# Feed-forward blocks of a two-part transformer: the first weight slice loaded a stage ahead, the gate folded into the down weights, and partition sums as float32r products

## The chip, the cores and the metric

The kernel runs on one core of a Trainium2 chip (trn2). The metric is device time in microseconds for one execution. A core has five engines with queues of their own: TensorE (PE, with its weight loads as PEld), VectorE (DVE), ScalarE (ACT), GpSimd (POOL) and SyncE (SP), which here issues most of the DMA transfers.

## What is computed

Two transformer parts run one after the other on 512 tokens of width 1024, in float32. The change touches the feed-forward block, which occurs twice in the first part, once behind a mixer of RWKV type (i = 0) and once behind one with sparse attention (i = 1):

```
def _swiglu(h, w_in, w_out):
    gate, up = jnp.split(h @ w_in, 2, axis=-1)
    return (jax.nn.silu(gate) * up) @ w_out
...
for i in range(DEPTH):
    mod = cond @ ada_w[i] + ada_b[i]
    sh1, sc1, gt1, sh2, sc2, gt2 = jnp.split(mod[:, None, :], 6, axis=-1)
    ...
    x = _layernorm(DEEPNORM_ALPHA * x + (1 + gt1) * y, ln_g[i, 0], ln_b[i, 0])
    hin = x * (1 + sc2) + sh2
    y = _swiglu(hin, ffn_w_in[i], ffn_w_out[i])
    x = _layernorm(DEEPNORM_ALPHA * x + (1 + gt2) * y, ln_g[i, 1], ln_b[i, 1])
```

The hidden width is 2816, that is 22 slices of 128. `cond` is silu of a vector of 1024, so `mod` is a matrix-vector product with a matrix of 1024 x 6144.

## The kernel before

The program is a row of stages: projections, chunks and end of the RWKV mixer ("proj", "chunks", "mixed"), feed-forward ("ffn0"), attention ("dsa"), feed-forward ("ffn1"), then the second part with "hyb" and the experts. Between two stages stands a barrier of all engines. `stay` holds the tiles that outlive a stage. Within a stage every engine has a list of its own, written by hand, and semaphores tie them together; the order on an engine is the order of the code.

Float32 products run as three float32r products: each operand is split into a high part (a cast) and a low part (`low_half`, a subtraction), and `matmul_halves` adds high x high, low x high and high x low (lines 49 to 51).

`swiglu` does one feed-forward block:

- **Input.** TensorE transposes `x` into eight chunks, ScalarE scales and shifts them (line 300, `xT`), VectorE splits them (lines 381 and 43). Between the fourth and the fifth chunk (`FIRST = 3`) both engines take in the first slice's weights (`cast_in`, `split_in`).
- **Gate and up.** For each slice n of 128 hidden columns SP loads 1 MB of weights (`load_in`, two transfers, line 169), ScalarE casts them (line 296), VectorE makes the low half, TensorE runs 2 x 8 x 3 products of 128x512, ScalarE applies silu (line 312), VectorE multiplies and splits the result (`gate_up`, lines 361, 363, 43). Weights have two buffers, `wi[0]` and `wi[1]`.
- **The next modulation.** Beside this the block computes `mod` of the layer that follows, in 24 pieces of 256 columns. SP loads 1 MB per piece (line 163), VectorE sums 8 terms into `nsum` and adds the bias on one partition (`next_piece`, lines 371 to 377), TensorE sums over the partitions with a product against a column of ones (`next_sum`, line 230), ScalarE copies the row out and stores it. The first pair of slices (`pair(0)`) handles two pieces per slice, the loop behind it one.
- **Down.** 22 slices of `w_out`, 0.5 MB each, go through a ring of four buffers (line 198). VectorE casts and subtracts (`split_out`, lines 351 and 43). Eight PSUM banks collect 4 quarters of tokens x 2 halves of columns. Up to slice 17 TensorE takes all quarters of a slice, the last four slices quarter by quarter.
- **End.** `deepnorm_rows` works off the quarters on VectorE: gate times bank (line 431), plus ALPHA times x (432), moments (434), normalisation (439, 440). The mixers end with the same function.

The down buffers lie on the same memory as the gate/up buffers.

## Time and profile before

| | us |
|---|---|
| median of 3 runs | 2979.43 |
| the runs | 2970.38, 2979.43, 2979.59 |
| profiled execution, own time | 2968.92 |
| its span, first to last instruction | 2967.2 |
| busy in it: TensorE / VectorE / ScalarE | 2613.1 / 1962.0 / 908.8 |
| first feed-forward block | 639 to 1051 |
| second feed-forward block | 1376 to 1791 |

Times in rows count from the span's start. A row of the timeline gives start, duration, engine, line, operation, what is written and read, and in brackets the idle time before it with what ended it. Rows of one engine can overlap a little, since a duration includes the way through the pipeline; the step from start to start is what counts. Busy time is an average over many stages; what a change in a stage is worth shows in who waits for whom there. In row names both feed-forward blocks read `ffn`.

### The profile page before, as it was taken

How to read it: one execution, taken by the hardware profiler on the slowest of the kernel's cores; microseconds unless marked ns; L12 is line 12 of the kernel's file. 1: busy time of each engine (PE TensorE's matmuls, PEld its weight loads, DVE VectorE, ACT ScalarE, POOL GpSimd, SP SyncE). 2: the span in 40 equal slices, each digit the busy share in tenths (PEclk: the TensorE clock that was granted, in tenths of full speed). 3: DMA queues.
4: the chain of work that ended last, by engine and by line, in shares of the span. 5: the costliest groups of instructions: out<-in, count | busy, mean ns of one | idle time of the engine just before them, and what ended most of it. 6: DMA issues, size and time to landing. Idle time of an engine off the chain costs nothing. (4 is left out here: it accounts for less than half of the span.)

```text
span 2967.2 us, 41251 instructions
## 1 busy us (share of the span) xinstructions
PE 2613.1 (88%) x16553; PEld 1913.8 (65%) x16553; DVE 1962.0 (66%) x2648; ACT 908.8 (31%) x961; POOL 409.6 (14%) x214
## 2 busy tenths in 40 slices
PE   5999888869999979996999996998882899999991
PEld 3444888447778744663777875885432688888880
DVE  7580666777764538526776457976524799999983
ACT  2201111122220022522222003333101677777761
POOL 0000000100000010000000000000001266666642
PEclk8999999989999989998999998999995899999995
DMA  5210222226663270102665323220306699999962
GB/s 186 85 57 18 93 74 74 115 92 199 186 182 99 85 252 29 58 29 93 202 188 175 100 85 112 87 86 29 142 8 218 237 361 368 369 359 360 355 246 102
DMA packets 241388, 459.54 MB, mean 155 GB/s; under 512 B 30966, under 2 KB 193294, under 8 KB 225897
## 3 DMA queue, kind: packets, MB, share of 16 engines
q1 hardware_dynamic: 220344, 432.09, 41.9%
q0 software_dynamic: 14368, 23.79, 2.3%
q10 hardware_dynamic: 6546, 1.79, 0.3%
q8 instruction: 99, 1.62, 0.2%
q14 instruction: 31, 0.25, 0.0%
HBM read 457.49 MB, written 30.56 MB: 164 GB/s over the span
## 5 line engine op out<-in xcount | busy, mean ns | idle before, releaser
L49 PE MATMUL ffn_bank<-ffn_xT_high,ffn_wi_high 128*128 128x512 f32 x704 | 281.2, 399 | 20.7 <-ACT ffn_xT L300 18.2
L50 PE MATMUL ffn_bank<-ffn_xT_low,ffn_wi_high 128*128 128x512 f32 x704 | 275.9, 392 | 0.0
L51 PE MATMUL ffn_bank<-ffn_xT_high,ffn_wi_low 128*128 128x512 f32 x704 | 275.9, 392 | 0.0
L296 ACT CAST ffn_wi_high<-ffn_wi 128x2048 fp32r<-128x2048 f32 x44 | 84.0, 1910 | 355.1 <-DMA ffn_wi<-in_ffn_w_in 320.9
L49 PEld LDWEIGHTS ffn_bank<-ffn_xT_high,ffn_wi_high 128*128 128x128 f32 x704 | 133.3, 189 | 66.1 <-ACT ffn_xT L300 18.6
L374 DVE SCALAR_TENSOR_TENSOR ffn_nsum<-ffn_nw,ffn_cond,ffn_nsum 128x256 f32<-128x256 f32 x336 | 163.0, 485 | 12.0
L2810 POOL DMA_INDIRECT expert_rows<-exp_ys,exp_to_row x32 | 155.6, 4863 | 45.1 <-issue 44.3
L43 DVE TENSOR_TENSOR moe_g_low<-moe_g,exp_g_high 128x4096 fp32r<-128x4096 f32 x32 | 141.6, 4425 | 30.0 <-ACT exp_g_high L2884 30.0
L43 DVE TENSOR_TENSOR ffn_wi_low<-ffn_wi,ffn_wi_high 128x2048 fp32r<-128x2048 f32 x44 | 100.8, 2291 | 79.9 <-ACT ffn_wi_high L296 79.9
L51 PEld LDWEIGHTS ffn_bank<-ffn_xT_high,ffn_wi_low 128*128 128x128 f32 x704 | 133.3, 189 | 28.7
L2884 ACT CAST exp_g_high<-moe_g 128x4096 fp32r<-128x4096 f32 x32 | 116.3, 3634 | 113.1 <-PE exp_p_g L51 83.6
L43 DVE TENSOR_TENSOR moe_u_low<-moe_u,exp_u_high 128x4096 fp32r<-128x4096 f32 x32 | 141.6, 4426 | 13.6 <-ACT exp_u_high L2884 13.6
L50 PEld LDWEIGHTS ffn_bank<-ffn_xT_low,ffn_wi_high 128*128 128x128 f32 x704 | 133.3, 189 | 26.5
L43 DVE TENSOR_TENSOR moe_d_low<-moe_d,exp_d_high 128x4096 fp32r<-128x4096 f32 x32 | 141.4, 4419 | 0.0
L49 PE MATMUL ffn_bank<-ffn_wo_high,ffn_act_high 128*128 128x512 f32 x352 | 137.4, 390 | 2.4 <-DVE ffn_wo_low L43 2.4
L50 PE MATMUL ffn_bank<-ffn_wo_low,ffn_act_high 128*128 128x512 f32 x352 | 137.0, 389 | 0.0
L51 PE MATMUL ffn_bank<-ffn_wo_high,ffn_act_low 128*128 128x512 f32 x352 | 137.0, 389 | 0.0
L2884 ACT CAST exp_d_high<-moe_d 128x4096 fp32r<-128x4096 f32 x32 | 116.5, 3642 | 2.1 <-DMA moe_d<-in_w_e_down 2.1
L2794 POOL COPY exp_from_row<-exp_rows 128x2 int32 (+1 forms) x30 | 113.9, 3796 | 19.4 <-PE exp_p_x L2839 19.2
L351 DVE CAST ffn_wo_high<-ffn_wo 128x1024 fp32r<-128x1024 f32 x44 | 30.5, 694 | 129.9 <-DMA ffn_wo<-in_ffn_w_out 129.9
L2884 ACT CAST exp_u_high<-moe_u 128x4096 fp32r<-128x4096 f32 x32 | 116.4, 3636 | 0.0
L49 PE MATMUL exp_p_g<-exp_g_high,exp_xT_high 128*128 128x512 f32 x256 | 105.6, 412 | 8.4 <-DVE exp_xT_low L43 8.4
(608 smaller groups left out, 5937.7 us busy)
## 6 DMA issues: line engine op xcount, KB each, us to landing
moe_g<-in_w_e_gate SPq DMA_DIRECT2D x32, 2048.0 KB, 9.5
moe_u<-in_w_e_up SPq DMA_DIRECT2D x32, 2048.0 KB, 10.0
moe_d<-in_w_e_down SPq DMA_DIRECT2D x32, 2048.0 KB, 9.3
ffn_wi<-in_ffn_w_in SPq DMA_DIRECT2D x88, 512.0 KB, 5.2
ffn_nw<-in_ada_w SPq DMA_DIRECT2D x24, 1024.0 KB
ffn_nw<-in_w_ada SPq DMA_DIRECT2D x24, 1024.0 KB
ffn_wo<-in_ffn_w_out SPq DMA_DIRECT2D x44, 512.0 KB, 3.3
hyb_wb<-in_w_in SPq DMA_DIRECT2D x20, 1024.0 KB, 5.9
```

What stands on the lines that cost most here:

```text
L43: return engine.tensor_tensor(low, x, high.bitcast(F32), ALU.subtract)
L49: nc.tensor.matmul(out, w[0], x[0], start=start, stop=False, **kw)
L50: nc.tensor.matmul(out, w[0], x[1], start=False, stop=False, **kw)
L51: return nc.tensor.matmul(out, w[1], x[0], start=False, stop=stop, **kw)
L296: nc.scalar.copy(wi_high[h][:, :, :, :], wi[h][:, :, :, :]).then_inc(s["wi_highs"], 1)
L351: nc.vector.tensor_copy(wo_high[slot][:, :], wo[slot][:, :]).then_inc(s["wo_highs"], 1)
L374: nc.vector.scalar_tensor_tensor(out=total, in0=nw[:, b, k, :], scalar=cond[:, k:k + 1], in1=total, op0=ALU.mult, op1=ALU.add).then_inc(s[ ...
L2794: nc.gpsimd.tensor_copy(from_row[h][:, :, :], rows[:, bass.ds(n, 1), :]).then_inc(s["from_copied"], 1)
L2810: nc.gpsimd.indirect_dma_start(ys_dram, bass.IndirectOffsetOnAxis(ap=to_row[h][:, 0, 1:2].bitcast(U32), axis=0), ys[h][:, :], None, bounds ...
L2884: nc.scalar.copy(flat(high_of(name, h)[:, :, :]), flat(raw[name][h][:, :, :])).then_inc(s[f"{name}_high"], 1)
```

## The change

Three things, all in the feed-forward blocks:

1. A tile `z` (8 KB per partition, float32, with `z_r` as its float32r view) joins `stay` and takes the place of `wi[0]`. The stage ahead of each block loads the first slice's weights into it: the last stage of the RWKV mixer behind its other loads, the attention stage behind its output weights and a wait on `prep_psum`. Other stages keep tiles of their own in `z` (`kk` and `sq`, `RBB`, `w_uk` and `w_uv`, a third ring buffer, `xg`). ScalarE and VectorE take in slice 0 ahead of all eight chunks.
2. The partition sum becomes two float32r products with 128x128 ones; VectorE makes `nsum_high` and `nsum_low` for it.
3. The gate plus one is formed at the start of the block and multiplied into each slice of down weights; `deepnorm_rows` skips its multiplication there. The rooms move: the first two down buffers and `g`, `b` lie on `nw` now, so their loads wait for the last piece (`nsum_done`).

```diff
+def load_first_slice(engine, stay, w_in, z_loaded):
+    for part in range(2):
+        engine.dma_start(first_slice(stay["z"])[:, part, :, :],
+                         w_in.rearrange("(p k) n -> p k n", k=KD)[:, :, part * FFN:part * FFN + P]).then_inc(z_loaded, 16)
...
-                load_in(0, 0)
                 load_in(1, 1)
                 load_piece(0, 0)
                 load_piece(1, 1)
...
-                    if f == 0 or f == 2:
-                        sp.wait_ge(s["hidden"], 2 * (NF - 1) + f)
-                        sp.wait_ge(s["wi_split"], NF - 1 + f // 2)
+                    if f == 0:
+                        sp.wait_ge(s["nsum_done"], PIECES + 1)
+                    if f == 2:
+                        sp.wait_ge(s["hidden"], 2 * NF)
...
-                pool.dma_start(gt[:, :], spread(gate)).then_inc(s["v_loaded"], 16)
+                pool.dma_start(gt[:, :], spread(gate)).then_inc(s["gt_loaded"], 16)
+                pool.wait_ge(s["nsum_done"], PIECES + 1)
                 pool.dma_start(g[:, :], spread(ln_g)).then_inc(s["v_loaded"], 16)
...
-                    nc.tensor.matmul(bank[4 + b][0:1, 0:PIECE], ones[:, :], nsum[:, b, :], start=True, stop=True).then_inc(s["n_psum"], 1)
+                    nc.tensor.matmul(bank[4 + b][:, 0:PIECE], ones[:, :], nsum_high[:, b, :], start=True, stop=False)
+                    nc.tensor.matmul(bank[4 + b][:, 0:PIECE], ones[:, :], nsum_low[:, b, :], start=False, stop=True).then_inc(s["n_psum"], 1)
...
+                cast_in(0, 0)
                 for k in range(KD):
                     act.wait_ge(s["xT_psum"], k + 1)
...
-                    if k == FIRST:
-                        cast_in(0, 0)
...
                     dve.wait_ge(wo_loaded[slot], f // WO_RING * 16 + 16)
+                    nc.vector.tensor_tensor(wo[slot][:, :], wo[slot][:, :], gt[:, :], ALU.mult).then_inc(s["wo_gated"], 1)
+                    dve.wait_ge(s["wo_gated"], f + 1)
                     nc.vector.tensor_copy(wo_high[slot][:, :], wo[slot][:, :]).then_inc(s["wo_highs"], 1)
...
-                    nc.vector.tensor_tensor(total[0:1, :], total[0:1, :], nbias[:, b, :], ALU.add).then_inc(s["nsum_done"], 1)
+                    nc.vector.tensor_tensor(total[0:1, :], total[0:1, :], nbias[:, b, :], ALU.add).then_inc(s["nsum_biased"], 1)
+                    dve.wait_ge(s["nsum_biased"], p + 1)
+                    nc.vector.tensor_copy(nsum_high[:, b, :], total).then_inc(s["nsum_high"], 1)
+                    dve.wait_ge(s["nsum_high"], p + 1)
+                    low_half(nc.vector, nsum_low[:, b, :], total, nsum_high[:, b, :]).then_inc(s["nsum_done"], 1)
...
+                split_in(0, 0)
                 for k in range(KD):
...
                 split_in(1, 1)
+                dve.wait_ge(s["gt_loaded"], 16)
+                link(nc.vector.tensor_scalar(gt[:, :], gt[:, :], 1.0, None, ALU.add))
...
@@ deepnorm_rows
-            link(nc.vector.tensor_tensor(y[:, t, cols], bank_of(t, j)[:, :], gt[:, cols], ALU.mult))
-            link(nc.vector.scalar_tensor_tensor(out=y[:, t, cols], in0=x[:, t, cols], scalar=ALPHA, in1=y[:, t, cols],
+            branch = bank_of(t, j)[:, :]
+            if gt is not None:
+                link(nc.vector.tensor_tensor(y[:, t, cols], branch, gt[:, cols], ALU.mult))
+                branch = y[:, t, cols]
+            link(nc.vector.scalar_tensor_tensor(out=y[:, t, cols], in0=x[:, t, cols], scalar=ALPHA, in1=branch,
                                                 op0=ALU.mult, op1=ALU.add))
...
@@ rwkv_finish, SP
             sp.dma_start(x_first, x_in.rearrange("(t p) d -> p t d", p=P)).then_inc(loaded, 16)
+            load_first_slice(sp, stay, next_w_in, z_loaded)
...
@@ dsa, SP
                 sp.dma_start(w_out, w["w_out"].rearrange("(q p) n -> p q n", p=P)).then_inc(ring_loaded[1], 16)
+                sp.wait_ge(s["prep_psum"], 18)
+                load_first_slice(sp, stay, next_w_in, z_loaded)
                 sp.wait_ge(s["o_psum"], KD)
```

ScalarE at the start of a feed-forward block, before (`ffn_xT` are the chunks of the input, `ffn_wi_high` the cast weights):

```order
L300 ACTIVATE ffn_xT<-ffn_bank,stay_sh,stay_sc 128x512 x4
L296 CAST ffn_wi_high<-ffn_wi 128x2048
L300 ACTIVATE ffn_xT<-ffn_bank,stay_sh,stay_sc 128x512 x4
L305 ACT_TABLE_LOAD
L305 ACTIVATE ffn_sig<-ffn_cond 128x8
L296 CAST ffn_wi_high<-ffn_wi 128x2048
```

and after:

```order
L319 CAST ffn_wi_high<-stay_z 128x2048
L324 ACTIVATE ffn_xT<-ffn_bank,stay_sh,stay_sc 128x512 x8
L327 ACT_TABLE_LOAD
L327 ACTIVATE ffn_sig<-ffn_cond 128x8
L319 CAST ffn_wi_high<-ffn_wi 128x2048
```

The first cast has moved from the middle of the chunks ahead of them, and reads `z`.

VectorE at the same place, from the last chunk through the first two pieces, before:

```order
L381 CAST ffn_xT_high<-ffn_xT 128x512
L43 TENSOR_TENSOR ffn_xT_low<-ffn_xT,ffn_xT_high 128x512
L43 TENSOR_TENSOR ffn_wi_low<-ffn_wi,ffn_wi_high 128x2048
L387 TENSOR_TENSOR ffn_cond<-ffn_cond,ffn_sig 128x8
L371 TENSOR_SCALAR ffn_nsum<-ffn_nw,ffn_cond 128x256
L374 SCALAR_TENSOR_TENSOR ffn_nsum<-ffn_nw,ffn_cond,ffn_nsum 128x256 x7
L377 TENSOR_TENSOR ffn_nsum<-ffn_nsum,ffn_nbias 1x256
L371 TENSOR_SCALAR ffn_nsum<-ffn_nw,ffn_cond 128x256
L374 SCALAR_TENSOR_TENSOR ffn_nsum<-ffn_nw,ffn_cond,ffn_nsum 128x256 x7
L377 TENSOR_TENSOR ffn_nsum<-ffn_nsum,ffn_nbias 1x256
```

and after, the first of the two pieces:

```order
L410 CAST ffn_xT_high<-ffn_xT 128x512
L43 TENSOR_TENSOR ffn_xT_low<-ffn_xT,ffn_xT_high 128x512
L43 TENSOR_TENSOR ffn_wi_low<-ffn_wi,ffn_wi_high 128x2048
L414 TENSOR_SCALAR ffn_gt<-ffn_gt 128x1024
L416 TENSOR_TENSOR ffn_cond<-ffn_cond,ffn_sig 128x8
L395 TENSOR_SCALAR ffn_nsum<-ffn_nw,ffn_cond 128x256
L398 SCALAR_TENSOR_TENSOR ffn_nsum<-ffn_nw,ffn_cond,ffn_nsum 128x256 x7
L401 TENSOR_TENSOR ffn_nsum<-ffn_nsum,ffn_nbias 1x256
L403 CAST ffn_nsum_high<-ffn_nsum 128x256
L43 TENSOR_TENSOR ffn_nsum_low<-ffn_nsum,ffn_nsum_high 128x256
```

The gate's plus one has come in ahead of `cond`, and a cast and a subtraction end every piece.

TensorE between slices 0 and 1, before:

```order
L50 MATMUL ffn_bank<-ffn_xT_low,ffn_wi_high 128x512
L51 MATMUL ffn_bank<-ffn_xT_high,ffn_wi_low 128x512
L230 MATMUL ffn_bank<-ffn_nsum,ffn_ones 1x256 x2
L49 MATMUL ffn_bank<-ffn_xT_high,ffn_wi_high 128x512
L50 MATMUL ffn_bank<-ffn_xT_low,ffn_wi_high 128x512
```

and after:

```order
L51 MATMUL ffn_bank<-ffn_xT_high,stay_z_r 128x512
L249 MATMUL ffn_bank<-ffn_nsum_high,ffn_ones 128x256
L250 MATMUL ffn_bank<-ffn_nsum_low,ffn_ones 128x256
L249 MATMUL ffn_bank<-ffn_nsum_high,ffn_ones 128x256
L250 MATMUL ffn_bank<-ffn_nsum_low,ffn_ones 128x256
L49 MATMUL ffn_bank<-ffn_xT_high,ffn_wi_high 128x512
```

Two float32r products stand where one fp32 product stood, for each of the two pieces here.

## Rows read from the trace of the kernel before

**Rows 1.** The page's header: the span of the profiled execution.
```profile
span 2967.2 us, 41251 instructions
```
**Rows 2.** Timeline of ScalarE, first block, around the first cast of weights.
```profile
647.82 1.90 ACT L296 CAST ffn_wi_high<-ffn_wi 128x2048 fp32r<-128x2048 f32 x1 [3.98 <-DMA ffn_wi<-in_ffn_w_in]
649.63 2.78 ACT L300 ACTIVATE ffn_xT<-ffn_bank,stay_sh,stay_sc 128x512 f32<-128x512 f32 x4
```
**Rows 3.** Timeline of VectorE, first block: its waits up to slice 2.
```profile
641.32 0.43 DVE L381 CAST ffn_xT_high<-ffn_xT 128x512 fp32r<-128x512 f32 x1 [1.70 <-ACT ffn_xT L300]
...
649.75 2.29 DVE L43 TENSOR_TENSOR ffn_wi_low<-ffn_wi,ffn_wi_high 128x2048 fp32r<-128x2048 f32 x1 [4.09 <-ACT ffn_wi_high L296]
...
679.28 2.29 DVE L43 TENSOR_TENSOR ffn_wi_low<-ffn_wi,ffn_wi_high 128x2048 fp32r<-128x2048 f32 x1 [1.35 <-ACT ffn_wi_high L296]
```
**Rows 4.** Timeline of VectorE, second block: the wait for the first weights.
```profile
1389.86 2.29 DVE L43 TENSOR_TENSOR ffn_wi_low<-ffn_wi,ffn_wi_high 128x2048 fp32r<-128x2048 f32 x1 [7.97 <-ACT ffn_wi_high L296]
```
**Rows 5.** Timeline of TensorE, first block: its waits, and a late partition sum.
```profile
652.46 0.79 PE L49 MATMUL ffn_bank<-ffn_xT_high,ffn_wi_high 128*128 128x512 f32 x1 [6.59 <-ACT ffn_xT L300]
...
667.48 0.59 PE L230 MATMUL ffn_bank<-ffn_nsum,ffn_ones 128*1 128x256 f32 x2 [1.98 <-DVE ffn_nsum L377]
...
694.33 0.50 PE L49 MATMUL ffn_bank<-ffn_xT_high,ffn_wi_high 128*128 128x512 f32 x1 [0.88 <-DVE ffn_wi_low L43]
...
879.93 0.59 PE L230 MATMUL ffn_bank<-ffn_nsum,ffn_ones 128*1 128x256 f32 x2
...
880.45 0.50 PE L49 MATMUL ffn_bank<-ffn_xT_high,ffn_wi_high 128*128 128x512 f32 x1
880.79 0.39 PE L50 MATMUL ffn_bank<-ffn_xT_low,ffn_wi_high 128*128 128x512 f32 x1
```
**Rows 6.** Windows: us, PE busy (count), granted clock, DMA share, GB/s.
```profile
655.00:657.00 2.00, 2.00 (x9) 0.91 1.10 349
669.00:670.00 1.00, 1.00 (x4) 0.51 0.93 266
670.00:672.00 2.00, 2.00 (x6) 0.50 1.03 350
```
**Rows 7.** Timeline, stage "hyb": float32r products of 128x256 and a weight load.
```profile
1910.03 0.28 PE L50 MATMUL hyb_bank<-hyb_wb_low,stay_h_high 128*128 128x256 f32 x1
1910.03 0.19 PEld L51 LDWEIGHTS hyb_bank<-hyb_wb_high,hyb_hT_low 128*128 128x128 f32 x1
1910.14 0.28 PE L51 MATMUL hyb_bank<-hyb_wb_high,hyb_hT_low 128*128 128x256 f32 x1
```
**Rows 8.** Groups by line and shape, VectorE: busy us, mean ns of one.
```profile
L351 DVE CAST ffn_wo_high<-ffn_wo 128x1024 fp32r<-128x1024 f32 x44 | 30.5, 694 | 129.9 <-DMA ffn_wo<-in_ffn_w_out 129.9
L381 DVE CAST ffn_xT_high<-ffn_xT 128x512 fp32r<-128x512 f32 x16 | 6.7, 421 | 3.4 <-ACT ffn_xT L300 3.4
L43 DVE TENSOR_TENSOR ffn_wo_low<-ffn_wo,ffn_wo_high 128x1024 fp32r<-128x1024 f32 x44 | 53.9, 1225 | 1.5
L43 DVE TENSOR_TENSOR ffn_xT_low<-ffn_xT,ffn_xT_high 128x512 fp32r<-128x512 f32 x16 | 11.1, 692 | 0.5
L374 DVE SCALAR_TENSOR_TENSOR ffn_nsum<-ffn_nw,ffn_cond,ffn_nsum 128x256 f32<-128x256 f32 x336 | 163.0, 485 | 12.0
```
**Rows 9.** Timeline: VectorE's tail, first block; TensorE's last wait, second block.
```profile
1019.96 0.69 DVE L431 TENSOR_TENSOR ffn_y<-ffn_bank,ffn_gt 128x512 f32<-128x512 f32 x1 [0.35 <-PE ffn_bank L51]
...
1027.71 0.68 DVE L431 TENSOR_TENSOR ffn_y<-ffn_bank,ffn_gt 128x512 f32<-128x512 f32 x1
...
1759.06 0.50 PE L49 MATMUL ffn_bank<-ffn_wo_high,ffn_act_high 128*128 128x512 f32 x1 [1.24 <-DVE ffn_wo_low L43]
```
**Rows 10.** Timeline of VectorE, first block, steady slices.
```profile
729.00 0.69 DVE L361 TENSOR_TENSOR ffn_hid<-ffn_sil,ffn_bank 128x512 f32 x1 [0.52 <-PE ffn_bank L51]
...
880.23 0.69 DVE L361 TENSOR_TENSOR ffn_hid<-ffn_sil,ffn_bank 128x512 f32 x1 [1.46 <-PE ffn_bank L51]
...
888.24 2.29 DVE L43 TENSOR_TENSOR ffn_wi_low<-ffn_wi,ffn_wi_high 128x2048 fp32r<-128x2048 f32 x1 [1.69 <-ACT ffn_wi_high L296]
```

More of the change, by code:

```diff
@@ L104, in swiglu @@
     WO_RING = 4
-    FIRST = 3
     STEADY = NF - WO_RING
@@ L111, in swiglu @@
         room = Room(nc, ctx, phase)
-        nw = room.sb("nw", [P, 2, KD, PIECE])
         xT_high, y = room.shared(("xT_high", [P, KD, T], F32R), ("y", [P, NT, D], F32))
@@ L478, in rwkv_project @@
     hid = room.sb("hid", [P, 2, T])
-    kk = room.sb("kk", [P, 2, T])
-    sq = room.sb("sq", [P, 2, T])
+    kk, sq = (stay["z"][:, n * 2 * T:(n + 1) * 2 * T].rearrange("p (a t) -> p a t", a=2) for n in range(2))
     nrm = room.sb("nrm", [P, 2, T])
@@ L866, in rwkv_chunks @@
     MK = room.sb("MK", [P, 2, KD, 2, CHUNK])
-    RBB = room.sb("RBB", [P, 2, KD, 2, CHUNK])
+    RBB = stay["z"][:, :].rearrange("p (e q k t) -> p e q k t", e=2, q=KD, k=2)
     ZA = room.sb("ZA", [P, 2, KD, 2, CHUNK])
@@ L1903, in hybrid @@
         xn = sgb[:, :, :].rearrange("p (t a) n -> p t (a n)", t=NT)
-        *third, hm = room.shared(("wb2", [P, KD, WB], F32), ("wb_low2", [P, KD, WB], F32R), ("hm", [P, NT, M_INNER], F32))
+        third = [stay[n][:, :].rearrange("p (k n) -> p k n", k=KD) for n in ("z", "z_r")]
+        hm = stay["z"][:, :].rearrange("p (t n) -> p t n", t=NT)
         wb, wb_low = zip(*raw_low, third)
@@ L2722, in experts @@
     rows = room.sb("rows", [P, UNITS, 2], I32)
-    xg = [room.sb(f"xg{i}", [P, D]) for i in range(2)]
+    xg = [stay["z"][:, i * D:(i + 1) * D] for i in range(2)]
     xT_high = room.sb("xT_high", [P, KD, P], F32R)
@@ L3064, in two_blocks @@
                                            ("h_high", [P, KD, T], F32R), ("x", [P, NT, D], F32))))
+        stay.update(zip(("z", "z_r"), room.shared(("z", [P, 2 * KD * P], F32), ("z_r", [P, 2 * KD * P], F32R))))
+        z_loaded = [nc.alloc_semaphore(f"z_loaded{n}") for n in range(2)]
         stay.update(ident=room.sb("ident", [P, P]), sc=room.sb("sc", [P, KD]), sh=room.sb("sh", [P, KD]))
```

63 lines of the change are left out of this document (36 added, 27 removed).

## Prediction

> **What bounds the kernel now.** The page's header comes first: one execution spans 2967.2 us [rows 1]. The change works in the two feed-forward blocks, from 639 to 1051 us and from 1376 to 1791 us, so only they are read. The question in each is who makes whom wait, and it has three answers.
>
> At the start TensorE waits. ScalarE converts the first slice's weights between the fourth and the fifth chunk of the transposed input; that conversion waits for a load that was only issued when the block began, and the last four chunks stand behind it [rows 2]. TensorE's first product starts at 652.46 after 6.59 us of waiting [rows 5]. VectorE waits too: 1.70 us for the first chunk, 4.09 us for the first converted weights, 1.35 us for those of slice 2 [rows 3]. In the second block the load takes longer, and the middle wait is 7.97 us [rows 4]; the other two are as in the first, 1.70 and 1.39. But look at what TensorE waits for next: at 667.48 for VectorE's partition sum of piece 1, and at 694.33 for VectorE's low half of slice 3's weights [rows 5]. The loop's first pair does two pieces per slice instead of one, and up to slice 3 the limit is VectorE's own queue.
>
> From slice 3 on TensorE is the limit. VectorE's gate step at the end of a slice stands at 729.00 and 13 slices later at 880.23, which is 11.63 us per slice. The low half of the next weights starts at 888.24 and takes 2.29, so it is done at 890.5, some 1.5 us before TensorE begins on it at about 892 [rows 10].
>
> At the end VectorE is the limit: each quarter of the tokens costs it 1027.71 - 1019.96 = 7.75 us [rows 9], while TensorE needs 4 x 6 products of about 0.23 us, 5.4 us.
>
> **Part 1, the early load.** The wait of ScalarE goes, and the conversion (1.90) comes ahead of the eight chunks instead of among them: it ends at about 641.3, the chunks go at 0.70 apiece (2.78 for four [rows 2]), so TensorE can start at about 647.0, 5.5 us earlier; in the second block some 9. That is not the gain. Up to slice 3 VectorE decides, so I add up VectorE's queue. It loses the waits of 4.09 and 1.35 us. The latter goes because slice 2's load is issued behind piece 1, which is done earlier, while VectorE arrives with more work behind it. The 1.70 stays, now as the wait for ScalarE's conversion. Added is, in each of six pieces before slice 3, a cast and a subtraction of 128x256. No row shows either on this tile. Cast: 0.421 for 512 and 0.694 for 1024 elements give 0.285 for 256. Subtraction: 0.692 and 1.225 give 0.425; the nearest row of this size, with a scalar, is 0.485 [rows 8]. With 0.03 for each new wait on the step before, 0.77 per piece, 4.6 for six; bounds 0.5 (both hidden in part behind the previous step's end) and 1.1 (0.421 + 0.692). The gate's plus one, 0.69 + 0.03, now also stands there. So slice 3 starts by -4.09 - 1.35 + 4.6 + 0.72 = **-0.1 us** in the first block and -7.97 - 1.39 + 5.3 = **-4.0 us** in the second. What hides the second slice's load is that it is now first in SP's queue, with 1 MB less ahead and 1 MB (scale and shift of the norm) moved to the block's end; if it still landed as late as 1387.9, some 1.5 us of the 4.0 would go.
>
> TensorE's waits do not vanish, they move. Piece 1 comes only 4.09 - 0.72 - 1.54 = 1.8 us earlier, while slice 0 ends over 5 us earlier; and before slice 3 the wait of 0.88 [rows 5] grows to about 2.9, since slice 2 starts up to 1.8 earlier and slice 3's weights come when they came before. After a wait of 1.98 us (667.48) the granted clock fell to 0.51 at 669 and stayed at 0.50 to 672 [rows 5, 6]: some 3.2 us at 1.2 GHz instead of 2.4, a loss of 1.6. The wait of 0.88 had none behind it. I expect such a stretch in slice 3 of both blocks, where nothing covers it: **+3.2 us**, bounds 0 and 6.4 (twice as long).
> On this the Trainium skill (TensorE: Matmul & The Clock Gate, HAM oscillation) says that a burst behind a long wait for data starts at the half rate again; by that rule the 3.2 stand, without it the sum would be 3.2 lower. The row at 669 agrees with it.
>
> The two extra DMA issues stand at the end of SP's queue in the mixer's last stage, behind everything it loads, and in the attention stage behind the output weights, with only a reload of the input behind them that waits for much later work. I cost them at nothing; 1 MB among 8, if it held up the x load, would be 3 to 5 us once, and VectorE takes x up tens of us later.
>
> **Part 2, partition sums as float32r.** Today one fp32 product with one column of weights runs as two instructions: from 879.93 to the next slice's product 0.52 us, which itself is followed by the next only after 0.34 [rows 5]. After, two products of 128x256 in float32r. The mixer of the second block runs such products at 0.11 apart, with their 128x128 weight loads alongside [rows 7]. Of the 0.52 some 0.43 is array time and becomes 0.23: 0.20 saved, with bounds 0 and 0.31 (if the slow first product behind it goes too). It counts where TensorE is the limit, behind slices 3 to 21, 19 times in each block: **-7.6 us**, bounds 0 and -11.8. The 20 or so slices each give VectorE 0.77 more; it has 1.46 us of idle time before the gate step and 1.69 before the low half [rows 10], so TensorE hides it.
> Against this part speaks a rule of the Trainium skill (TensorE: Matmul & The Clock Gate, LDWEIGHTS): a weight load costs by its columns, so 128 columns instead of 1. If the two loads stood in the open at the 0.107 us that it gives, an estimate from that page, the saving would be nil and the sum 7.6 higher. The rows of the 128x256 stream show them hidden.
>
> **Part 3, the gate in the down weights.** VectorE gets 22 more multiplications of 128x1024, 1.225 each [rows 8]: 3.2 us per slice of weights instead of 1.9, against TensorE's 5.4. Hidden, except for the last one: slice 21's load is issued only when TensorE leaves slice 17, and TensorE already waits 1.24 us for its low half [rows 9]. That wait grows by 1.23 + 0.03: **+2.5 us** over two blocks. The scale's plus one leaves this place, but it lay in that wait. In return the tail loses eight multiplications per block, each 0.69 with 0.03 to the step that depends on it, 0.72 [rows 9]: **-11.6 us** for sixteen. VectorE then takes 6.3 us per quarter and is still behind TensorE's 5.4, so all of it counts. The step that now reads PSUM keeps its length: the multiplication, which read the bank, took as long. The loads of the first two down slices come earlier, into the room of the next modulation's weights; TensorE did not wait for them before, so nothing.
>
> **The sum** is -4.1 + 3.2 - 7.6 + 2.5 - 11.6 = **-17.6 us**. The profiled execution took 2968.9 (span 2967.2 and 1.7 around it), so 2951.3 on its terms. The three timed runs were 2970.4, 2979.4 and 2979.6: the profiled one lies at the lower end. Against the median of 2979.4 the forecast is **2962 us**; if most runs fall on the lower level, 2953.
>
> **Rivals.** *The start pays in full* (0.10): VectorE's queue isn't the limit up to slice 3, and TensorE keeps its 5.5 and 9. For it: ScalarE's wait is the visible one. Against it: TensorE's waits at 667.48 and 694.33, both for VectorE. Then the start gives -14.5 instead of -0.9: 2948.
> *The small products and steps give nothing* (0.15): the weight loads stand open, or the added VectorE steps cost 1.1 instead of 0.77 (+2 per block, and slice 3 later still). Then -17.6 + 7.6 + 4 = -6: 2973, no difference that can be told.
> *Slower, by the clock* (0.05): behind the longer waits of both first slices TensorE stays at 1.2 GHz for a whole slice of 48 products, 10.9 us more each, instead of 1.6. In slice 1 about 3 of that is covered by VectorE's work, in slice 3 nothing: some 8 + 10.9 per block, 38 in all, less the 21 that the other terms give: +17, 2996. It decides from the point where the low stretches cost more than the other terms give, 10 us per block. Against it: after the wait of 6.59 us that ended at 652.46 the granted clock was back at 0.91 between 655 and 657, and the stretch from 669 ends behind 672 [rows 5, 6].
>
> **Numbers.** The forecast has 0.70. The range from 2946 to 2973 takes in the lower level of the runs with the full start, and the case in which the small steps give nothing. About 0.3%, 9 us, is what a measurement of this kernel can tell from no change: faster 0.82, same 0.13, slower 0.05.
>
> **What the profile after would show.** Right: the first product near 647 (first block), TensorE waiting 5 us for the sum of piece 1 and near 3 us for slice 3's low half, slice 3 starting within 1 us of 694.3; a step from slice to slice of 11.4 instead of 11.63 us; two and a half us of wait for the last down slice; a tail quarter of 6.3. Wrong: slice 3 near 689 (the first rival), slices still 11.6 apart (the second), a granted clock of 0.5 for whole slices (the third). A wait of the tail for TensorE would make part 3 worth less.

## The result, and the profile after

| us | before | after |
|---|---|---|
| median of the timed runs | 2979.43 | 2952.51 |
| lowest run | 2970.38 | 2945.45 |
| profiled execution, own time | 2968.92 | 2955.74 |
| its span | 2967.2 | 2954.0 |
| first block, start to end | 411.59 | 400.26 |
| second block, start to end | 415.56 | 401.47 |
| attention stage between them | 324.6 | 334.6 |

The ratio after to before is 0.9915, 95% interval 0.9893 to 0.9937: about 25 us faster (19 to 32). One of the five runs after, 4086.52 us at a mean granted clock of 0.614 where the others have 0.94, is a slow run and left out of the ratio; the median of the other four is 2949.0. On another chip 11 runs before and 6 after gave medians of 2970.03 and 2950.02, ratio 0.9936 (0.9924 to 0.9948), which is 20 us. In the profiled pair the two blocks give 11.33 + 14.09 = 25.4 us, and the attention stage, which the change doesn't touch, takes 10.0 back; the experiments show that this is not the change.

The page's header:
```profile
span 2954.0 us, 41412 instructions
```
The start. Timelines of ScalarE and VectorE, first block (start, duration, engine, line, operation, idle time before it); compare [rows 2, 3]:
```profile
640.33 1.90 ACT L319 CAST ffn_wi_high<-stay_z 128x2048 fp32r<-128x2048 f32 x1 [4.14 <-PEq L86]
642.13 5.76 ACT L324 ACTIVATE ffn_xT<-ffn_bank,stay_sh,stay_sc 128x512 f32<-128x512 f32 x8
```
```profile
642.26 2.29 DVE L43 TENSOR_TENSOR stay_z_r<-stay_z,ffn_wi_high 128x2048 fp32r<-128x2048 f32 x1 [1.53 <-ACT ffn_wi_high L319]
...
655.19 0.69 DVE L414 TENSOR_SCALAR ffn_gt<-ffn_gt 128x1024 f32<-128x1024 f32 x1
...
660.59 0.29 DVE L403 CAST ffn_nsum_high<-ffn_nsum 128x256 fp32r<-128x256 f32 x1
660.92 0.43 DVE L43 TENSOR_TENSOR ffn_nsum_low<-ffn_nsum,ffn_nsum_high 128x256 fp32r<-128x256 f32 x1
...
692.76 2.29 DVE L43 TENSOR_TENSOR ffn_wi_low<-ffn_wi,ffn_wi_high 128x2048 fp32r<-128x2048 f32 x1
```
The weights are there: ScalarE converts them first and takes the eight chunks in a row. VectorE has no bracket behind 642.26: it never waits up to slice 3, its queue is full. TensorE, first block, its waits; compare [rows 5]:
```profile
647.95 0.50 PE L49 MATMUL ffn_bank<-ffn_xT_high,ffn_wi_high 128*128 128x512 f32 x1 [1.10 <-ACT ffn_xT L324]
...
666.55 0.58 PE L249 MATMUL ffn_bank<-ffn_nsum_high,ffn_ones 128*128 128x256 f32 x1 [4.64 <-DVE ffn_nsum_low L43]
...
695.10 0.50 PE L49 MATMUL ffn_bank<-ffn_xT_high,ffn_wi_high 128*128 128x512 f32 x1 [2.68 <-DVE ffn_wi_low L43]
```
Counted from the block's start its first product comes 5.5 us earlier (7.56 us into the block instead of 13.05), and it gives this back at 666.55 and 695.10. In the second block the wait before slice 3 is as long, but the clock falls behind it. Windows (us, TensorE busy and count, granted clock, DMA share, GB/s): first block, second block:
```profile
697.00:700.00 3.00, 3.00 (x14) 1.00 1.11 328
1432.00:1434.00 2.00, 2.00 (x7) 0.50 1.09 307
```
The steady slices. TensorE from one slice to the next, and VectorE's gate steps (both first block); compare [rows 5, 10]:
```profile
762.70 0.39 PE L51 MATMUL ffn_bank<-ffn_xT_high,stay_z_r 128*128 128x512 f32 x1
762.93 0.28 PE L249 MATMUL ffn_bank<-ffn_nsum_high,ffn_ones 128*128 128x256 f32 x1
763.04 0.28 PE L250 MATMUL ffn_bank<-ffn_nsum_low,ffn_ones 128*128 128x256 f32 x1
763.16 0.39 PE L49 MATMUL ffn_bank<-ffn_xT_high,ffn_wi_high 128*128 128x512 f32 x1
763.39 0.39 PE L50 MATMUL ffn_bank<-ffn_xT_low,ffn_wi_high 128*128 128x512 f32 x1
```
```profile
864.26 0.69 DVE L385 TENSOR_TENSOR ffn_hid<-ffn_sil,ffn_bank 128x512 f32 x1 [0.58 <-PE ffn_bank L51]
875.59 0.69 DVE L385 TENSOR_TENSOR ffn_hid<-ffn_sil,ffn_bank 128x512 f32 x1 [0.56 <-PE ffn_bank L51]
886.72 0.69 DVE L385 TENSOR_TENSOR ffn_hid<-ffn_sil,ffn_bank 128x512 f32 x1 [0.92 <-PE ffn_bank L51]
```
The two products stand 0.11 apart, and no gap is left around them: from the start of the slice's last product (762.70) to the next slice's first (763.16) it is 0.46 us, and the one after that follows at 0.23. The steps from gate to gate alternate, 11.33 and 11.13 us, where before they were 11.63.

The end. TensorE's wait for the last down slice (first block), and two quarters of the tail on VectorE; compare [rows 9]:
```profile
1013.61 0.50 PE L49 MATMUL ffn_bank<-ffn_wo_high,ffn_act_high 128*128 128x512 f32 x1 [2.45 <-DVE ffn_wo_low L43]
```
```profile
1028.00 0.68 DVE L462 SCALAR_TENSOR_TENSOR ffn_y<-stay_x,ffn_bank 128x512 f32<-128x512 f32 x1
...
1034.28 0.68 DVE L462 SCALAR_TENSOR_TENSOR ffn_y<-stay_x,ffn_bank 128x512 f32<-128x512 f32 x1
```
The wait has grown by 1.2 us, and a quarter takes 6.28 us instead of 7.75. Behind the longer wait the granted clock fell in this block (window as above):
```profile
1016.00:1018.00 2.00, 2.00 (x7) 0.50 0.00 0
```

### The profile page after: what moved, and what is told of

Its sections match the earlier page's. It is cut to its first block and busy times, and to the rows that moved or that the text cites. A ratio compares the mean times of both kernels' runs of the same rounds, so it can differ in the third digit from the quotient of the medians.

```text
span 2954.0 us, 41412 instructions
## 1 busy us (share of the span) xinstructions
PE 2612.4 (88%) x16553; PEld 1938.3 (66%) x16553; DVE 2038.8 (69%) x2772; ACT 910.4 (31%) x961; POOL 409.0 (14%) x214
## 5 line engine op out<-in xcount | busy, mean ns | idle before, releaser
L51 PE MATMUL ffn_bank<-ffn_xT_high,ffn_wi_low 128*128 128x512 f32 x352 | 139.2, 395 | 0.0
L51 PE MATMUL ffn_bank<-ffn_xT_high,stay_z_r 128*128 128x512 f32 x352 | 139.1, 395 | 0.0
L49 PE MATMUL exp_p_y<-exp_d_high,exp_aT_high 128*128 128x512 f32 x256 | 104.9, 410 | 6.7 <-DVE moe_d_low L43 6.7
L373 DVE TENSOR_TENSOR ffn_wo<-ffn_wo,ffn_gt 128x1024 f32<-128x1024 f32 x44 | 53.9, 1225 | 77.3 <-DMA ffn_wo<-in_ffn_w_out 77.3
L49 PE MATMUL hyb_bank<-stay_h_high,hyb_wb_high 128*128 128x512 f32 x256 | 103.6, 405 | 1.2 <-DVE hyb_wb_low L43 1.2
```

Of the source, the lines that this page charges most:

```text
L49: nc.tensor.matmul(out, w[0], x[0], start=start, stop=False, **kw)
L51: return nc.tensor.matmul(out, w[1], x[0], start=False, stop=stop, **kw)
L373: nc.vector.tensor_tensor(wo[slot][:, :], wo[slot][:, :], gt[:, :], ALU.mult).then_inc(s["wo_gated"], 1)
```

## The experiments

Each block is measured at five points of its own time, counted from VectorE's first instruction in it: the gate step before slice 3 ("to slice 3"), that of slice 3, the 18 steps from slice 3's to slice 21's ("18 steps"), from there to the first step of the tail ("down"), and the tail. First block / second block, and the attention stage between them:

| us | to slice 3 | slice 3 | 18 steps | down | tail | block | attention |
|---|---|---|---|---|---|---|---|
| before | 54.79 / 58.71 | 11.54 / 11.55 | 209.20 / 209.20 | 105.02 / 105.06 | 31.04 / 31.04 | 411.59 / 415.56 | 324.6 |
| after | 54.57 / 54.62 | 11.58 / 13.17 | 202.43 / 202.67 | 105.75 / 105.79 | 25.93 / 25.22 | 400.26 / 401.47 | 334.6 |
| fp32_sum | 51.67 / 51.27 | 11.54 / 11.55 | 210.82 / 210.82 | 106.24 / 106.23 | 25.22 / 25.94 | 405.49 / 405.81 | 336.5 |
| gate_tail | 54.58 / 54.58 | 11.56 / 11.58 | 202.19 / 202.70 | 104.43 / 104.49 | 31.05 / 31.05 | 403.81 / 404.40 | 337.9 |
| late_load | 57.21 / 59.57 | 13.13 / 13.20 | 201.88 / 202.86 | 105.60 / 105.70 | 25.21 / 25.21 | 403.03 / 406.54 | 324.9 |
| light_pieces | 48.78 / 48.77 | 11.12 / 11.55 | 203.32 / 204.24 | 106.16 / 105.63 | 25.48 / 25.22 | 394.86 / 395.41 | 325.1 |
| one_column | 54.57 / 54.58 | 11.57 / 13.15 | 202.93 / 202.03 | 105.82 / 105.67 | 25.90 / 25.94 | 400.79 / 401.37 | 325.2 |
| pe_double | 54.56 / 54.69 | 12.93 / 13.19 | 203.78 / 203.27 | 105.73 / 105.73 | 25.21 / 25.93 | 402.21 / 402.81 | 336.7 |
| mixed_sums | 52.40 / 52.12 | 11.57 / 11.55 | 202.29 / 203.25 | 105.68 / 106.19 | 25.88 / 25.67 | 397.82 / 398.78 | 325.1 |
| ordered | 54.53 / 55.10 | 12.90 / 13.20 | 201.88 / 202.72 | 105.72 / 105.77 | 25.89 / 25.96 | 400.92 / 402.75 | 334.6 |
| order_only | 57.49 / 57.65 | 13.57 / 13.38 | 202.92 / 202.78 | 105.70 / 105.70 | 25.91 / 25.85 | 405.59 / 405.36 | 325.2 |
| swapped | 59.61 / 58.42 | 13.27 / 13.31 | 203.06 / 203.01 | 105.72 / 105.71 | 25.87 / 25.95 | 407.53 / 406.40 | 334.6 |
| after_again | 54.57 / 54.57 | 13.18 / 12.93 | 202.31 / 202.26 | 105.72 / 105.98 | 25.91 / 25.74 | 401.69 / 401.48 | 322.8 |
| before_again | 55.94 / 57.69 | 11.55 / 11.54 | 209.20 / 209.46 | 104.96 / 104.92 | 31.05 / 31.05 | 412.70 / 414.66 | 336.3 |

The first column can be split further. It is VectorE's waits up to slice 3 (the brackets in its timeline, each at least 0.15 us) and the rest, which is VectorE's own work with the shorter gaps in it:

| us | waits | work |
|---|---|---|
| before | 7.14 / 11.06 | 47.65 / 47.65 |
| before_again | 8.14 / 10.06 | 47.81 / 47.63 |
| after | 1.53 / 1.53 | 53.05 / 53.08 |
| late_load | 3.97 / 6.24 | 53.24 / 53.33 |
| fp32_sum | 3.38 / 2.99 | 48.28 / 48.28 |
| light_pieces | 4.87 / 4.84 | 43.92 / 43.93 |
| mixed_sums | 3.12 / 2.84 | 49.28 / 49.27 |
| order_only | 4.27 / 4.44 | 53.22 / 53.21 |

A single execution's time moves by 10 to 14 us with the attention stage, in which no arithmetic is edited; so the experiments are read in the blocks. The 18 steps hold a few single ones that are up to 1.0 us longer (in the longest TensorE waited 1.1 us for a low half); without such steps the 18 take 201.9 us in the changed kernel (late_load, first block).

**fp32_sum: the partition sums as before.**
```diff
-        ones = room.sb("ones", [P, P], F32R)
+        ones = room.sb("ones", [P, 1])
-                    nc.tensor.matmul(bank[4 + b][:, 0:PIECE], ones[:, :], nsum_high[:, b, :], start=True, stop=False)
-                    nc.tensor.matmul(bank[4 + b][:, 0:PIECE], ones[:, :], nsum_low[:, b, :], start=False, stop=True)...
+                    nc.tensor.matmul(bank[4 + b][0:1, 0:PIECE], ones[:, :], nsum[:, b, :], start=True, stop=True)...
```
(and without the cast and the subtraction of a piece on VectorE)

> The changed kernel with part 2 undone: one fp32 product with a column of ones again, and no cast and subtraction at the end of a piece. Theory: TensorE's cost between slices is the fp32 pair and its surroundings, so the step from gate step to gate step goes back from 11.12/11.33 to 11.63 us in every slice, 7 us per block; VectorE's queue ahead of slice 3 loses 6 x 0.77 us, so slice 3's gate step comes at about 50.0 us after the block's start instead of 54.6. Sum per block +2 to +3 us against the changed kernel (400.3 and 401.5 from the block's start to its end). Rival, that the early load and the moved loads made the slices shorter: the steps stay at 11.12/11.33 and the block gets 4.6 us shorter.

Time 2966.22. The block is 5.2 and 4.3 us longer than after. The 18 steps take 8.4 and 8.2 us more, 0.46 each; the slices up to slice 3 take 2.9 and 3.4 less. VectorE is rid of twelve small instructions there, 4.8 us of work, but a part comes back as a wait for slice 2's converted weights, first block:
```profile
676.80 2.29 DVE L43 TENSOR_TENSOR stay_z_r<-stay_z,ffn_wi_high 128x2048 fp32r<-128x2048 f32 x1 [1.71 <-ACT ffn_wi_high L318]
```
So the float32r sums win 8.9 and 8.6 us in the steady part (with 0.5 and 0.4 behind slice 21) and pay 3 for it at the start. In the second block they pay 1.6 more in slice 3: TensorE's wait before it is 0.79 us here and 2.64 in after, and only behind the longer one the granted clock fell. TensorE, first block; the fp32 product starts 0.32 behind the last one of the slice, takes 0.52, and is followed by a slow product of 0.34:
```profile
772.98 0.39 PE L51 MATMUL ffn_bank<-ffn_xT_high,ffn_wi_low 128*128 128x512 f32 x1
773.30 0.59 PE L249 MATMUL ffn_bank<-ffn_nsum,ffn_ones 128*1 128x256 f32 x2
773.82 0.50 PE L49 MATMUL ffn_bank<-ffn_xT_high,ffn_wi_high 128*128 128x512 f32 x1
774.16 0.39 PE L50 MATMUL ffn_bank<-ffn_xT_low,ffn_wi_high 128*128 128x512 f32 x1
```
Yet the steps are not back at 11.63: they alternate between 11.82 and 11.63. Something else in the change makes every second slice 0.2 us slower.

**gate_tail: the gate multiplied in the tail again.**
```diff
-                    nc.vector.tensor_tensor(wo[slot][:, :], wo[slot][:, :], gt[:, :], ALU.mult).then_inc(s["wo_gated"], 1)
-                    dve.wait_ge(s["wo_gated"], f + 1)
-                deepnorm_rows(nc, dve, link, lambda t, j: bank[2 * t + j], s["y_psum"], x, None, y, g, b, ...
+                deepnorm_rows(nc, dve, link, lambda t, j: bank[2 * t + j], s["y_psum"], x, gt, y, g, b, ...
```


> The changed kernel with part 3 undone in its arithmetic: the gate multiplies the eight half rows at the end again, the down weights are only split; all loads and rooms stay as changed. Theory: the stretch from the first of the tail's steps to the block's end goes from 25.2 to 25.9 back to 31.0 us, TensorE's wait for the last down slice from 2.45 back to 1.24. Sum per block about +4.2 us. Rival, that the multiplications in the down weights slow TensorE elsewhere: more than 1.3 us comes back ahead of the tail.

Time 2959.95; the blocks are 3.6 and 2.9 us longer than after. The tail is 31.05 again and TensorE's wait for the last down slice 1.13 and 1.22; "down" is 1.3 us shorter, the price of the last slice's multiplication (forecast 1.26). TensorE's wait, second block:
```profile
1752.70 0.50 PE L49 MATMUL ffn_bank<-ffn_wo_high,ffn_act_high 128*128 128x512 f32 x1 [1.22 <-DVE ffn_wo_low L43]
```
The tail's gain is 5.8 where the clock is full and 5.1 where it isn't. In the first block of after the granted clock fell behind the longer wait at 1013.61, so that VectorE had to wait for the second quarter (0.61 us, for TensorE). Over all runs the clock fell behind this wait in 16 of the 22 blocks in which it was 2.1 to 2.6 us, and in none of the 6 (before, before_again, gate_tail) in which it was 1.1 to 1.2.

**late_load: the first slice's weights loaded when the block begins.**
```diff
+                for part in range(2):
+                    sp.dma_start(wi[0][:, part, :, :], w_in_v[:, :, part * FFN:part * FFN + P]).then_inc(z_loaded, 16)
-                cast_in(0, 0)
                 for k in range(KD):
+                    if k == 3:
+                        cast_in(0, 0)
```
(the same for VectorE's `split_in`; the loads in the stages before are gone)

> The changed kernel with part 1 undone: the first slice's weights are loaded when the block begins, and both engines take them in between the fourth and fifth chunk. Theory, VectorE's queue decides until slice 3: slice 3's gate step moves by VectorE's regained wait, about +4 to +5.5 us in the first block (54.6 to 59 or 60) and +8 to +9.4 in the second; TensorE's first product comes 5.5 and 9 us later, and its waits of 4.6 us for the sum of piece 1 and 2.7 for slice 3's weights shrink. Rival, TensorE's start decides: slice 3 moves by the full shift of the first product in both blocks and TensorE's later waits stay as long.

Time 2954.90. Slice 3 comes 2.6 and 5.0 us later, not 4 to 5.5 and 8 to 9.4. The forecast took VectorE's waits from before; in this execution the load came sooner. VectorE's wait for the first converted weights, first and second block:
```profile
651.55 2.29 DVE L43 TENSOR_TENSOR stay_z_r<-stay_z,ffn_wi_high 128x2048 fp32r<-128x2048 f32 x1 [2.40 <-ACT ffn_wi_high L321]
1381.78 2.29 DVE L43 TENSOR_TENSOR stay_z_r<-stay_z,ffn_wi_high 128x2048 fp32r<-128x2048 f32 x1 [4.68 <-ACT ffn_wi_high L321]
```
Without them slice 3 comes 2.6 and 5.0 us earlier: the early load is worth in full what VectorE would have waited. How much that is differs from execution to execution, since the late load arrives when it likes. ScalarE's first conversion starts 8.4 and 12.3 us into the block in before, 9.0 and 11.3 in before_again, 6.7 and 9.0 here, 9.0 and 8.1 in swapped, which loads late too.

**light_pieces: VectorE's work up to slice 3 cut.** Six pieces do four of their eight terms; the kernel leaves out the rest of the next layer's modulation there.

> The changed kernel, with the last four of the eight terms left out of the sums of the six pieces ahead of slice 3 (a one-element step stands in their place), so that the next layer's modulation is incomplete. This takes some 0.4 us x 4 x 6 = 9 to 10 us off VectorE's queue and nothing else. Theory: slice 3's gate step comes 9 to 10 us earlier in both blocks, at about 45 us after the start, where TensorE's own 3 x 11.2 us behind its start at 6.7 us sets a floor of about 43; TensorE's waits of 4.6 and 2.7 us nearly vanish. Rival, that loads or TensorE decide until slice 3: it stays within 2 us of 54.6.

Time 2933.09. The gain is 5.8 us, not 9 to 10. VectorE, first block:
```profile
675.76 2.29 DVE L43 TENSOR_TENSOR stay_z_r<-stay_z,ffn_wi_high 128x2048 fp32r<-128x2048 f32 x1 [2.42 <-ACT ffn_wi_high L319]
...
689.75 0.69 DVE L385 TENSOR_TENSOR ffn_hid<-ffn_sil,ffn_bank 128x512 f32 x1 [0.58 <-PE ffn_bank L51]
```
VectorE's queue is the limit by a few us only. It has 9.1 us less work, and 3.3 of that come back as waits: 2.4 us for slice 2's weights, and in the first block 0.58 for TensorE at slice 2's gate step.

**one_column: one column of ones as weights instead of 128.**
```diff
-                    nc.tensor.matmul(bank[4 + b][:, 0:PIECE], ones[:, :], nsum_high[:, b, :], start=True, stop=False)
+                    nc.tensor.matmul(bank[4 + b][0:1, 0:PIECE], ones[:, 0:1], nsum_high[:, b, :], start=True, stop=False)
```
(the low product likewise)

> The changed kernel with one edit: both float32r products of a partition sum use one column of ones as weights instead of 128, so that the sum lands in one partition. If the 128-column weight loads are hidden behind the products, as I take it, the steps from slice to slice stay as they are, 11.12 and 11.33 us in turn. If part of a load stands in the open, the steps get shorter by 0.05 to 0.2 us, 1 to 4 us per block.

Time 2944.32, with the attention stage at 325.2. The steps are 11.33 and 11.11: 0.01 less at most. The loads of 128 columns are hidden. The rule of the Trainium skill that was held against this part (TensorE: Matmul & The Clock Gate, LDWEIGHTS: a load costs by its columns) has no effect on the time here.

**pe_double: TensorE's loop with half as many branches.**
```diff
-                with pe.Fori(1, PAIRS) as i:
-                    pair(i)
+                with pe.Fori(0, (PAIRS - 1) // 2) as j:
+                    pair(j * 2 + 1)
+                    pair(j * 2 + 2)
```


> The changed kernel with one edit: TensorE's loop over pairs of slices runs 5 times over two pairs instead of 10 times over one. In the changed kernel every second step is 11.33 instead of 11.12 us, where TensorE's loop branch stands. If the branch is the 0.21 us, four of the ten such steps in a block go to 11.12 or so, with only every fourth step left at 11.33: 1.0 us less per block, 2 in all. If the longer step belongs to something else that alternates with the pair (the buffer in the shared room, the bank), nothing changes.

Time 2963.54, with the attention stage at 336.7. Every second step is still 11.33, also where no branch stands. The branch was the wrong suspect. What does go with the slow step is the tile that the slice reads: the slice that ends at 762.70 in after has its low half in `stay_z_r`. In it the 48 products start 10.87 us apart from first to last (751.83 to 762.70), in the next one, from `ffn_wi_low`, 10.66 (763.16 to 773.82). The difference is no single gap: averaged by their place in the slice, the steps from product to product are 0.224 to 0.241 us throughout the slow slices, and 0.226 to 0.228 behind the first step in the quick ones.

**swapped: the two weight buffers exchanged.**
```diff
-        wi, wi_low = zip([first_slice(stay[n]) for n in ("z", "z_r")], room.shared(("wi1", ...), ("wi_low1", ...)))
+        wi, wi_low = zip(room.shared(("wi0", ...), ("wi_low0", ...)), [first_slice(stay[n]) for n in ("z", "z_r")])
```
(on top of late_load)

> late_load with the two weight buffers exchanged: even slices' weights in a tile of the block, odd slices' weights in the memory that outlives the block (stay_z, stay_z_r), which in the changed kernel holds the even slices'. The changed kernel, fp32_sum, one_column and pe_double all have steps that alternate by 0.2 us, and the slower slice is the one whose low half is read from stay_z_r. If the place of the weights in memory is the cause, the alternation turns round: the steps of mean 11.23 stay, the slow slices are now the odd ones. If it is the parity of the slice (the PSUM banks, the loop), the even slices stay the slow ones.

The alternation turned round. In late_load the slow steps are those from slices 3 to 4, 5 to 6 and so on (11.33), the quick ones 11.12; here, in the second block, 4 to 5, 6 to 7 and so on are 11.34, the others 11.12. TensorE at the end of an odd slice, and the gate steps around it (first block):
```profile
760.34 0.39 PE L51 MATMUL ffn_bank<-ffn_xT_high,stay_z_r 128*128 128x512 f32 x1
```
```profile
749.63 0.69 DVE L388 TENSOR_TENSOR ffn_hid<-ffn_sil,ffn_bank 128x512 f32 x1 [1.02 <-PE ffn_bank L51]
760.97 0.69 DVE L388 TENSOR_TENSOR ffn_hid<-ffn_sil,ffn_bank 128x512 f32 x1 [1.10 <-PE ffn_bank L51]
772.09 0.69 DVE L388 TENSOR_TENSOR ffn_hid<-ffn_sil,ffn_bank 128x512 f32 x1 [0.95 <-PE ffn_bank L51]
```
So the pace goes with the pair of tiles and not with the slice's parity: 48 products take 0.21 us longer with the low half in `stay_z_r` than with it in a tile of the block, 1.6 us per block (fp32_sum against before, 18 steps). The swap moved float32 weights and low half together, so which of the two counts, and why, these runs don't tell. The time, 2969.00, is not compared further: this kernel has the late load, the low stretch in both blocks and that of the attention stage (334.6).

**mixed_sums: a version from what the runs showed.** The first four pieces' sums as one fp32 product each, without a cast; the gate's plus one behind slice 20's gate step; pe_double's loop.
```diff
+                    if isinstance(p, int):
+                        nc.tensor.matmul(bank[4 + b][0:1, 0:PIECE], one_column[:, :], nsum[:, b, :], start=True, stop=True)...
+                        return
                     nc.tensor.matmul(bank[4 + b][:, 0:PIECE], ones[:, :], nsum_high[:, b, :], start=True, stop=False)
...
-                link(nc.vector.tensor_scalar(gt[:, :], gt[:, :], 1.0, None, ALU.add))
                 dve.wait_ge(s["sig_done"], 1)
...
                 gate_up(NF - 2, 0)
+                link(nc.vector.tensor_scalar(gt[:, :], gt[:, :], 1.0, None, ALU.add))
```


> A version that should beat both kernels: the changed one with the doubled loop of pe_double, the sums of the first four pieces as one fp32 product each as before the change (these are the ones that VectorE's queue pays for: fp32_sum started slice 3 earlier by 2.9 us), and the gate's plus one behind slice 20's gate step, where VectorE waits 2.99 us for TensorE. VectorE's queue up to slice 3 gets 4 x 0.77 + 0.72 = 3.8 us shorter; TensorE's wait there is 2.7, so slice 3 starts some 2.7 us earlier; with 1.0 for the loop 3.7 per block, 7.4 in all against the changed kernel. If the start is held by another chain (the slices' own products and ScalarE's conversions), less than 2 per block comes of it.

Median 2942.82 (2941.62 to 2951.04), ratio to before 0.9916 (0.9902 to 0.9930); the changed kernel on the same chip (after_again) had 2950.02 (2945.43 to 2954.79) and 0.9936 (0.9924 to 0.9948). It is the best version here, by about 4 us from lowest to lowest, though the intervals overlap. The medians differ by 7.2, near the 7.4 forecast, but in the profiled pair not for its reasons: the loop gives nothing, the start gives 4.6 over both blocks, and 3.0 are luck, since behind a wait of 2.7 us before slice 3 the clock stayed full in both blocks here and fell in both of after_again. Against after slice 3 comes 2.2 and 2.5 us earlier, of 3.8 us of work taken from VectorE. The rest is a wait again. VectorE, ScalarE and SyncE, first block:
```profile
677.81 2.29 DVE L43 TENSOR_TENSOR stay_z_r<-stay_z,ffn_wi_high 128x2048 fp32r<-128x2048 f32 x1 [1.61 <-ACT ffn_wi_high L324]
```
```profile
675.87 1.91 ACT L324 CAST ffn_wi_high<-stay_z 128x2048 fp32r<-128x2048 f32 x1 [19.64 <-DMA stay_z<-in_ffn_w_in]
```
```profile
665.72 0.55 SPq L182 DMA_DIRECT2D ffn_nw<-in_ada_w  x1
666.31 0.50 SPq L183 DMA_DIRECT2D ffn_nbias<-in_ada_b  x1
666.86 1.41 SPq L188 DMA_DIRECT2D stay_z<-in_ffn_w_in  x2
```
Slice 2's weights are loaded behind piece 3, whose load waits for piece 1's sum, though their buffer has been free since slice 0 ended, nearly 6 us before.

**ordered and order_only: slice 2's weights ahead of piece 3.** With and without the edits of mixed_sums (its loop left out).
```diff
                             for b in range(2):
                                 sp.wait_ge(s["nsum_done"], 2 * h + b + 2)
                                 load_piece(2 * h + b + 2, b)
+                                if b == 0:
+                                    sp.wait_ge(s["hidden"], 2 * h + 2)
+                                    load_in(h + 2, h)
+                            continue
```


> A version that should beat the kernels so far. It is mixed_sums without the doubled loop of TensorE (which left the steps as they were), and with SyncE's queue in another order up to slice 3: slice 2's weights are loaded when slice 0's products are done, between the loads of pieces 2 and 3, and no longer behind piece 3, whose load waits for piece 1's sum. In mixed_sums VectorE waited 1.61 us for ScalarE's conversion of slice 2's weights, which had waited 19.64 us for this load. With the load some 5 us earlier that wait goes, and slice 3 starts 1.6 us earlier than in mixed_sums: its gate step at about 50.6 to 50.8 us after the block's start, 3.8 before the changed kernel's. Over both blocks 7.5 us less than the changed kernel. If a different chain holds slice 2, it stays at 52.2.

> The changed kernel with SyncE's new order alone. There VectorE comes to slice 2's low half at 678.48 without idle time, and ScalarE's conversion is done at 678.0: two chains of equal length. If VectorE's queue is the limit by itself, the earlier load brings nothing: slice 3's gate step stays at 54.6 us, within 0.3. If the load is the limit, it comes up to 4 us earlier.

Both got slower: ordered 2953.01 (2949.19 to 2958.00; ratio 0.9933, 0.9915 to 0.9951), its blocks 3.1 and 4.0 us longer than those of mixed_sums, though the intervals of the times overlap; order_only 2957.11, with slice 3 at 57.5 and its blocks 5.3 and 3.9 longer than those of after. The weights did come earlier, and the pieces later. VectorE in order_only, first block:
```profile
676.94 0.35 DVE L399 TENSOR_SCALAR ffn_nsum<-ffn_nw,ffn_cond 128x256 f32<-128x256 f32 x1 [0.70 <-DMA ffn_nbias<-in_ada_b]
...
693.36 0.35 DVE L399 TENSOR_SCALAR ffn_nsum<-ffn_nw,ffn_cond 128x256 f32<-128x256 f32 x1 [2.04 <-DMA ffn_nbias<-in_ada_b]
```
and in ordered:
```profile
673.79 0.35 DVE L404 TENSOR_SCALAR ffn_nsum<-ffn_nw,ffn_cond 128x256 f32<-128x256 f32 x1 [2.94 <-DMA ffn_nbias<-in_ada_b]
```
The two waits in order_only have two causes. Piece 3's load is issued as early as in after, 26.1 us into the block, but it now stands behind slice 2's megabyte. Piece 5's load stands behind slice 3's weights, and SyncE waits for the end of slice 1 before it issues those; so it goes out 41.3 us into the block instead of 38.2. SyncE in order_only, then in after:
```profile
683.20 1.25 SPq L187 DMA_DIRECT2D ffn_wi<-in_ffn_w_in  x2
684.49 1.05 SPq L181 DMA_DIRECT2D ffn_nw<-in_ada_w  x1
```
```profile
678.60 0.54 SPq L181 DMA_DIRECT2D ffn_nw<-in_ada_w  x1
679.18 0.50 SPq L182 DMA_DIRECT2D ffn_nbias<-in_ada_b  x1
679.73 1.75 SPq L187 DMA_DIRECT2D ffn_wi<-in_ffn_w_in  x2
```
The amount moved is not the limit by itself: up to slice 3 the DMA engines are busy 0.67 of the time (after, 640 to 695 us). A load moved ahead in SyncE's queue is paid by what stands behind it, and so is the wait that it brings along.

**after_again and before_again: the attention stage.**

> The changed kernel once more, unaltered, beside the others. The blocks should come out as before, 400.3 and 401.5 us. In the attention stage between the two blocks the profiled execution had the granted clock at 0.50 for 30 us; the stage took 334.6 us against 324.6. If that is a matter of the single execution, this one shows either 325 or 335, whatever the change; if it came with the change, it is 335 again.

> The kernel before, once more and unaltered. In its profiled execution the attention stage between the blocks took 324.6 us at the full granted clock. The executions of after, fp32_sum, gate_tail and pe_double had about 30 us at 0.50 there, those of late_load, light_pieces, one_column, mixed_sums and after_again had none, so I take it for a matter of the single execution. The kernel before then shows it too in some: this one comes out near 2969 (stage 325 us) or near 2980 (stage 335). A time near 2980 with the stage at 325 would speak against it.

after_again took 322.8 us there, before_again 336.3 (time 2981.06). Windows of TensorE 240.8 us behind the end of the first block: before_again, then after_again:
```profile
1295.00:1305.00 10.00, 9.32 (x44) 0.50 0.00 0
```
```profile
1283.53:1293.53 10.00, 8.42 (x47) 1.00 0.55 210
```
Both kernels do it in some executions, so it isn't the change. Of the 14 profiled executions the seven with 27 to 31 us at 0.50 in the middle of the stage are those in which it took 334.6 us or more; in the others it took 322.8 to 325.2. Outside the blocks before took 2140.0 us and after_again 2140.5; the two blocks of that pair differ by 24.0 us, the spans by 23.5.

## Why the prediction was right, and where its sum was not

The forecast was 2962 us, the median is 2952.5, inside the range and on the forecast's side. The sum was -17.6; the blocks gave -25.4 in the profiled pair and -24.0 in the pair of before and after_again, and the ratios of the timed runs say -25 on the first chip and -19 on the second.

- **The start** (-0.1 and -4.0): -0.2 and -4.1, and both halves are right. VectorE's waits up to slice 3 fell by 5.6 and 9.5 us (forecast 5.4 and 9.4), its work grew by 5.4 (forecast 5.3), and in after its only wait up to there is the 1.53 us before its first subtraction. What failed were the forecasts of the experiments, which took work away (fp32_sum, light_pieces, mixed_sums): of 4.8, 9.1 and 3.8 us only some 60 to 70% came, since waits came back, above all for ScalarE's conversion of slice 2's weights. That before waited so long in the second block is a matter of the execution: against before_again the start gives -1.4 and -3.1.
- **The clock** (+3.2): +1.6, in one block of two in after; in both blocks of after_again, +1.6 and +1.4. The size of a stretch was right, that it always comes was not: of the 14 blocks with a wait of 2.5 to 2.7 us before slice 3 (after, after_again, gate_tail, late_load, one_column, pe_double, mixed_sums) 8 show the low clock behind it and 6 don't; in swapped, ordered and order_only the wait is 2.8 to 5.2 us, and all 6 blocks show it. This bears on the rule weighed in the prediction (the Trainium skill, TensorE: Matmul & The Clock Gate, HAM oscillation): here a wait of 2.5 to 2.7 us for data made it possible and did not decide it.
- **The float32r sums** (-7.6): the term that was mis-sized. They save 0.46 to 0.49 per slice, not 0.20. With the fp32 product it was 0.32 + 0.52 + 0.34 = 1.18 us from the slice's last product to the second of the next; now it is 0.46 + 0.23 = 0.69. The working set 0.43 of array time (its own estimate; the rows show the 0.52 only) against 0.23 and left out what lay around it: 0.09 ahead of the product (0.32 where 0.23 is the usual step), 0.09 inside the 0.52, 0.11 in the slow product behind. The upper bound of 0.31 had only the last of these. Over both blocks it is 17.5 us. Against it stands what the prediction did not have at all, **the slower place of the weights**, +1.6 per block. By the table the steps give -13.3 and the stretch behind slice 21, in gate_tail, -1.2: net -14.5 (single longer steps in after cost some 1.3 of what it could be).
- **The last down slice** (+2.5): +2.6 by gate_tail. It shows as +1.5 in the table, since "down" also holds slice 21's sum.
- **The tail** (-11.6): -5.1 and -5.8. Right at full clock. The prediction priced the longer wait for the last down slice, but not the low stretch that can follow it: 0.3 to 0.8 us of the tail, in 16 of 22 blocks.

Together (start, clock, sums with the place, last slice, tail): -4.3 + 1.7 - 14.5 + 2.6 - 10.9 = -25.4. Of the rivals none came. Small products that give nothing are refuted by fp32_sum and one_column. A start that pays in full is refuted by slice 3 itself, at 54.6 us instead of 49, and by VectorE's timeline without a wait. TensorE slow for a whole slice is seen nowhere; the longest low stretch inside a slice is some 6 us (late_load, slice 1).
